# Beside a product-key layer: gates weighed on ScalarE and stored in pieces, table tiles split 56 and 72, and half of the value sums kept in PSUM

## The chip, the cores and the metric

One Trainium2 chip, one of its cores. The kernel is a single program that is launched once; the time is that of the device from the first to the last instruction and what lies around it, in microseconds (us), lower is better. "Before" is the kernel as it stood, "after" the kernel with the change.

## What is computed

The reference is one layer of an encoder: a token-mixing part (a long convolution, a dilated window attention, gates, an output projection and a layer norm), then a product-key retrieval over 16384 experts. Only the second part is touched:

```python
def peer(u, wq, keys, utab, vtab):              # 1024 tokens, width 1024
    q = (xt @ wq).reshape(T, 8, 2, 128)
    s = jnp.einsum('thpe,hpke->thpk', q, keys)
    sv, si = lax.top_k(s, 16)
    cand = (sv[:, :, 0, :, None] + sv[:, :, 1, None, :]).reshape(T, 8, 256)
    cidx = (si[:, :, 0, :, None] * 128 + si[:, :, 1, None, :]).reshape(T, 8, 256)
    tv, ti = lax.top_k(cand, 16)
    eidx = jnp.take_along_axis(cidx, ti, axis=-1)
    g = jax.nn.softmax(tv, axis=-1)
    ...
        a = jnp.einsum('cd,ced->ce', xb, utab[ib])
        coef = gb * jax.nn.gelu(a, approximate=False)
        return jnp.einsum('ce,ced->cd', coef, vtab[ib])
```

So each token has 8 x 16 = 128 chosen experts, each with a gate; the result is the gated sum of their rows of `vtab`, with a coefficient that needs the token's product with their rows of `utab`.

## The kernel before

The kernel treats 256 of the 1024 tokens sparsely (it gathers the chosen rows, one indirect DMA for each of 256 turns, 128 rows of 4 KB each) and 768 densely: for these it multiplies with the whole tables, 128 tiles of 128 experts. Every large product is done three times (`product3`, L79 to L81), since each f32 operand is held as a high and a low part.

Three stages at the end are touched.

**stage_select.** VectorE does the two rounds of top 16, the softmax and the indices for eight blocks of tokens, n = 0 to 7. Beside it TensorE works through the first tiles of `utab` (`se_aps`, 48 matmuls of 384 columns each tile): `AT` = 8 tiles for each block, so 64 in all. ScalarE rounds each tile to its high part (`k_ut_h`), GpSimd subtracts it (`k_ut_l`), ScalarE applies Gelu and stores the result to `scratch_ahead`. VectorE needs one exponential of ScalarE for each block; ScalarE does it behind tile `AT - 2` of the block.

**stage_gates.** TensorE does the other 64 tiles (`ga_aps`) and, beside them, writes the dense gate matrix. For each group of four tokens VectorE builds one-hot rows (`one_hot`): `second` marks the chosen second key, `first` the first key times the gate, in a high and a low f16 part. That is twelve instructions of 128 columns. TensorE multiplies them (eight small matmuls, `ga_ps`), ScalarE writes the group into a block buffer (`ga_wide` or `k_big` in turns), 12 groups to a block, 16 blocks. A whole block goes to `scratch_gates` in one DMA of 3072 KB, whose runs are 48 tokens x 4 B = 192 B long. Each tile has three groups. VectorE also does four products with gathered rows for each tile (`dot`, L1948) and the low part of the next tile (`low`, L1953). ScalarE issues both kinds of stores, `scratch_ahead` (L1908) and `scratch_gates` (L1912), from one queue in program order, and waits at those points like at any other instruction.

**stage_values.** 32 groups of four tiles. For each tile, VectorE multiplies Gelu by gate (`va_c`), ScalarE rounds the product and the tile of `vtab` (`va_c_h`, `va_vt_h`), VectorE makes the low parts (`va_c_l` L2148, `va_vt_l` L2152). TensorE then does, for each of `DT` = 6 tiles of tokens, 24 matmuls of 512 columns over the four tiles of the group, into one of four pairs of PSUM banks; VectorE adds each pair into `k_big` (`add_sums`, L2160): six adds in each group. TensorE starts a group when all four of its tiles are ready (`ready`) and finds a free pair by `f_ok`. On VectorE everything stands in one written order (`turn`): for t = 0 to 3 the product, one add, the two low parts of tile t of the next group, and two or three gathered rows (L2176); then the adds 4 and 5. Two groups are prepared in turns, so group g + 1 is prepared while TensorE does group g. The last two groups are multiplied into PSUM together, and the end adds the rest, the residual and the layer norm for eight tiles of tokens.

## Time and profile before

| | us |
|---|---|
| median of 3 runs | 4294.86 |
| lowest, highest | 4288.96, 4295.96 |
| the profiled execution | 4303.32 |
| its span, first to last instruction | 4301.5 |
| select, as TensorE sees it (1671.2 to 2208.2) | 537.0 |
| gates (2212.5 to 3178.3) | 965.8 |
| values, group 1 to 29 (3254.0 to 4204.6) | 950.6 |
| values, the rest to the end | 96.9 |

Over the span TensorE is busy for 88%, VectorE for 67%, ScalarE for 23% and GpSimd for 30%. These shares are a mean over stages with different limits. Times in the rows count from the span's start. A row of the timeline gives the start, the duration, the engine, the line, the instruction and, in brackets, how long the engine had been idle and who ended that. Instructions overlap with their successor, so what one costs in a chain is the distance from start to start, not the duration.

### The profile page before, as it was taken

What the parts mean: (1) busy time and instruction counts of PE and PEld (TensorE: products, weight loads), DVE (VectorE), ACT (ScalarE), POOL (GpSimd) and SP (SyncE); (2) the same over time, 40 slices, a digit from 0 to 9 for tenths busy, and PEclk for the clock granted to TensorE, in tenths of its full rate; (3) what the DMA queues carried; (4) which work ended last, traced back from release to release, by engine and by line L of the source; (5) the groups of instructions that cost most, each with busy time, mean ns of one, the idle gap of its engine ahead of it and who ended that gap; (6) DMA issues with size and microseconds to landing.
All of it is one profiled execution on the core that took longest, in us unless ns stands there. A gap on an engine that the chain in (4) does not pass through costs nothing. (4 is left out here: it accounts for less than half of the span.)

```text
span 4301.5 us, 57936 instructions
## 1 busy us (share of the span) xinstructions
PE 3764.7 (88%) x19170; PEld 3289.1 (76%) x19170; DVE 2871.9 (67%) x6317; ACT 977.2 (23%) x1361; POOL 1302.5 (30%) x805
## 2 busy tenths in 40 slices
PE   6889899997879798999987776777758999999997
PEld 3579788886757688999986776776757888888885
DVE  5562133224544315788778897988859888888898
ACT  1111122221132211222322222222222222222221
POOL 1132112112312112332333232323215544454450
PEclk9789999998989899999998898988889999999998
DMA  4741212216542223333349989898998787888784
GB/s 183 282 138 41 84 60 80 75 62 223 195 173 96 83 83 102 122 131 119 129 152 259 241 268 236 271 240 258 244 249 319 288 296 287 286 292 300 276 308 153
DMA packets 501996, 826.29 MB, mean 192 GB/s; under 512 B 288455, under 2 KB 309191, under 8 KB 495720
## 3 DMA queue, kind: packets, MB, share of 16 engines
q1 hardware_dynamic: 111848, 370.03, 24.8%
q0 software_dynamic: 84096, 318.80, 20.8%
q10 hardware_dynamic: 305856, 135.28, 13.1%
q8 instruction: 69, 1.13, 0.1%
q14 instruction: 127, 1.04, 0.1%
HBM read 679.31 MB, written 144.70 MB: 192 GB/s over the span
## 5 line engine op out<-in xcount | busy, mean ns | idle before, releaser
L2049 POOL DMA_INDIRECT va_rows<-in_vtab,k_pick x256 | 500.5, 1955 | 531.6 <-DVE k_big L2176 436.5
L79 PE MATMUL va_fps<-va_vt_h,va_c_h 128*128 128x512 f32 x1536 | 601.2, 391 | 53.8 <-DVE va_vt_l L2152 51.4
L80 PE MATMUL va_fps<-va_vt_l,va_c_h 128*128 128x512 f32 x1536 | 600.1, 391 | 0.0
L81 PE MATMUL va_fps<-va_vt_h,va_c_l 128*128 128x512 f32 x1536 | 599.7, 390 | 0.0
L79 PE MATMUL ga_aps<-k_u_h,k_ut_h 128*128 128x384 f32 x1024 | 382.4, 373 | 116.2 <-DVE k_ut_l L1953 112.2
L1941 DVE TENSOR_SCALAR ga_first<-ga_iota,k_sel,ga_gs 128x128 f16<-128x128 f16 x1536 | 427.9, 353 | 33.0 <-issue 33.0
L79 PEld LDWEIGHTS va_fps<-va_vt_h,va_c_h 128*128 128x128 f32 x1536 | 289.9, 189 | 116.9 <-DVE va_vt_l L2152 52.5
L80 PE MATMUL ga_aps<-k_u_l,k_ut_h 128*128 128x384 f32 x1024 | 367.8, 359 | 0.0
L81 PE MATMUL ga_aps<-k_u_h,k_ut_l 128*128 128x384 f32 x1024 | 366.8, 358 | 0.0
L79 PE MATMUL se_aps<-k_u_h,k_ut_h 128*128 128x384 f32 x1024 | 343.8, 336 | 15.2 <-POOL k_ut_l L1619 15.2
L80 PE MATMUL se_aps<-k_u_l,k_ut_h 128*128 128x384 f32 x1024 | 343.2, 335 | 0.0
L81 PE MATMUL se_aps<-k_u_h,k_ut_l 128*128 128x384 f32 x1024 | 343.2, 335 | 0.0
L81 PEld LDWEIGHTS va_fps<-va_vt_h,va_c_l 128*128 128x128 f32 x1536 | 289.9, 189 | 60.6
L80 PEld LDWEIGHTS va_fps<-va_vt_l,va_c_h 128*128 128x128 f32 x1536 | 289.9, 189 | 60.1
L2176 DVE SCALAR_TENSOR_TENSOR k_big<-va_rows,va_coef,k_big 128x1024 f32<-128x1024 f32 x254 | 316.9, 1281 | 17.2 <-DMA va_rows<-in_vtab,k_pick 15.6
L79 PEld LDWEIGHTS ga_aps<-k_u_h,k_ut_h 128*128 128x128 f32 x1024 | 213.9, 209 | 123.2 <-issue 96.8
L1619 POOL TENSOR_TENSOR k_ut_l<-k_ut,k_ut_h 128x1024 fp32r<-128x1024 f32 x65 | 176.3, 2713 | 399.2 <-ACT k_ut_h L1666 399.2
L2160 DVE TENSOR_TENSOR k_big<-k_big,va_fps 128x1024 f32<-128x1024 f32 x174 | 211.5, 1218 | 105.6 <-PE va_fps L81 105.3
L1845 POOL DMA_INDIRECT k_big<-in_urows,k_pick x128 | 170.8, 1335 | 301.0 <-DVE k_big L1948 295.8
L1868 PE MATMUL ga_ps<-ga_first,ga_second 128*128 128x128 f16 x1536 | 126.6, 229 | 135.2 <-DVE ga_first L1941 135.2
L1845 POOL DMA_INDIRECT ga_rows<-in_urows,k_pick x128 | 121.3, 948 | 368.7 <-DVE ga_rows L1948 357.8
L1868 PEld LDWEIGHTS ga_ps<-ga_first,ga_second 128*128 128x128 f16 x1536 | 92.4, 102 | 168.1 <-DVE ga_first L1941 150.0
(293 smaller groups left out, 8173.6 us busy)
## 6 DMA issues: line engine op xcount, KB each, us to landing
k_ut<-in_utab SPq DMA_DIRECT2D x129, 512.0 KB, 3.3
va_vt<-in_vtab SPq DMA_DIRECT2D x128, 512.0 KB, 6.7
va_c<-scratch_ahead SPq DMA_DIRECT2D x128, 384.0 KB, 4.8
va_wt<-scratch_gates SPq DMA_DIRECT2D x128, 384.0 KB, 5.6
hy_tab<-in_tab POOLq DMA_DIRECT2D x64, 512.0 KB, 5.1
sp_wada<-in_w_ada SPq DMA_DIRECT2D x24, 1024.0 KB, 8.8
scratch_ahead<-se_gelu_a ACTq DMA_DIRECT2D x64, 384.0 KB, 2.4
scratch_ahead<-ga_gelu_a ACTq DMA_DIRECT2D x64, 384.0 KB, 4.6
```

Of the source, the lines that this page charges most:

```text
L79: nc.tensor.matmul(out, w[0], x[0], start=first, stop=False)
L80: nc.tensor.matmul(out, w[0], x[1], start=False, stop=False)
L81: return nc.tensor.matmul(out, w[1], x[0], start=False, stop=last)
L1619: nc.gpsimd.tensor_tensor(ut_l[:, s, :, :], ut[:, s, :, :], ut_h[:, s, :, :].bitcast(F32), ALU.subtract).then_inc(ut_ok, 1)
L1845: nc.gpsimd.indirect_dma_start(got[q % SLOTS_G], None, T["urows"], picked(K, q)).then_inc(got_in[q % SLOTS_G], 16)
L1868: last = nc.tensor.matmul(ps[:, e, t * NK:(t + 1) * NK], second[:, e, t, :], first[:, e, part, t, :], start=part == 0, stop=part == 1)
L1941: last = v.tensor_scalar(first[:, b, part, t, :], iota[:, :], K["sel"][:, 0, at], gs[:, part, at], ALU.is_equal, ALU.mult)
L2049: nc.gpsimd.indirect_dma_start(got[:, q % SLOTS_G, :], None, vrows, picked(K, q)).then_inc(got_in[q % SLOTS_G], 16)
L2160: v.tensor_tensor(row, row, banks(DT * s + tt), ALU.add).then_inc(f_ok, 1)
L2176: v.scalar_tensor_tensor(out=sums[:, n, :], in0=got[:, k, :], scalar=share, in1=sums[:, n, :], op0=ALU.mult, op1=ALU.add).then_inc(row_use ...
```

## The change

It does five things.

1. `AT` is 7 instead of 8: select does 56 tiles, gates does 72. The exponential stands behind tile `AT - 3` = 4 of a block instead of 6.
2. In gates, the 192 groups are spread over 72 tiles (4 turns of 18 tiles, 48 groups and 64 gathered rows), so a tile has two or three groups.
3. VectorE writes `second` and a plain `first` (no gate): eight instructions for each group instead of twelve. ScalarE reads the plain row and multiplies it by the low and by the high part of the gate (`weigh`): eight instructions of 128 columns for each group, each with a scale that is read from a column of `gs`. They stand two groups ahead of the group that ScalarE writes out.
4. A finished block is stored in four DMAs of 768 KB (same 192 B runs), one behind each of the next four tiles' stores to `scratch_ahead`. The last block is cut as before.
5. In values, three of the six tiles of tokens (`STAY` = 3, tt = 0, 1, 2) stay in three pairs of PSUM banks for the whole stage and are never added by VectorE. The other three pass through the fourth pair, one after the other. TensorE alternates: passing 0, staying 0, passing 1, staying 1, passing 2, staying 2. VectorE has three adds in a group, at t = 0, 1, 2, and none at t = 3. In the residual a staying tile needs one instruction instead of two, and all residual steps now come after the last `turn`.

```diff
-AT = 8
+AT = 7
...
-                        if j == AT - 2:
+                        if j == AT - 3:
                             act.wait_ge(e_in, n + 1)
...
+            def weigh(m):
+                act.wait_ge(hot_ok, m + 1)
+                b = m % 4
+                for part in (1, 0):
+                    for t in range(G):
+                        at = m * G + t
+                        last = nc.scalar.activation(first[:, b, part, t, :], first[:, b, 0, t, :], ACT.Copy,
+                                                    scale=gs[:, part, at:at + 1])
+                last.then_inc(f_ok, 1)
...
+            for n in range(BESIDE):
+                i, q, a = n // TILES, n % TILES, n % 2
+                split(1 - a, n + 1, n // 2)
+                act.wait_ge(act_stored[a], 16 * (n // 2 + 1))
+                todo = list(groups_of(q))
+                for h in range(2):
+                    gelu(a, n, h)
+                    for b in (todo[:-1], todo[-1:])[h]:
+                        m = GROUPS * i + b
+                        if m + AHEAD < BLOCKS * BLOCK:
+                            weigh(m + AHEAD)
+                        if m % BLOCK == 0 and m // BLOCK >= 2:
+                            hold(act, K, stored[m // BLOCK % 2], 16 * PIECES * (m // BLOCK // 2))
+                        scatter_out(m)
+                        if m % BLOCK == BLOCK - 1 and m // BLOCK < BLOCKS - 1:
+                            waiting += [(m // BLOCK, c, m) for c in range(PIECES)]
+                act.wait_ge(gelu_ok, 2 * n + 6)
+                act.dma_start(S["ahead"][n + FIRST], gelu_a[:, a, :]).then_inc(act_stored[a], 16)
+                if waiting:
+                    block, c, m = waiting.pop(0)
+                    act.wait_ge(act_out, m + 5)
+                    store(block, NK // PIECES * c, NK // PIECES * (c + 1), stored[block % 2])
...
                 for t in range(G):
                     at = bass.ds(m * G + t, 1)
                     v.tensor_scalar(second[:, b, t, :], iota[:, :], K["sel"][:, 1, at], None, ALU.is_equal)
-                    for part in range(2):
-                        last = v.tensor_scalar(first[:, b, part, t, :], iota[:, :], K["sel"][:, 0, at],
-                                               gs[:, part, at], ALU.is_equal, ALU.mult)
-                last.then_inc(f_ok, 1)
+                    last = v.tensor_scalar(first[:, b, 0, t, :], iota[:, :], K["sel"][:, 0, at], None, ALU.is_equal)
+                last.then_inc(hot_ok, 1)
...
+            def group(s, g):
+                ready(g)
+                for j in range(STAY):
+                    passing(s, g, j)
+                    last = staying(s, j, False)
+                last.then_inc(group_mm, 1)
...
                 for t in range(GT):
                     coefficients(g + 1, t)
-                    add(t)
+                    if t < STAY:
+                        add(t)
                     coef_low(1 - s, g + 1, t)
                     value_low(1 - s, g + 1, t)
                     for j in range(take * t, take * t + take):
                         take_row(start, j, isinstance(start, int) and start == 0 and j < GATHERED)
-                for tt in range(GT, DT):
-                    add(tt)
...
             for t in range(GT):
                 coefficients(NG - 1, t)
-                residual(DT - GT + t)
+                residual(t)
                 coef_low(1, NG - 1, t)
                 value_low(1, NG - 1, t)
```

ScalarE in gates, one tile with three groups. L1883 is the rounding of the next tile, L1893 Gelu, L1887 the writing out of a group. Before:

```order
L1883 ACTIVATE k_ut_h<-k_ut 128x1024
L1892 REGISTER_ALU
L1893 ACTIVATE ga_gelu_a<-ga_aps 128x384
L72 ISA
L1887 ACTIVATE ga_wide<-ga_ps 128x128x4
L72 REGISTER_ALU
L1887 ACTIVATE ga_wide<-ga_ps 128x128x4
L1892 REGISTER_ALU
L1893 ACTIVATE ga_gelu_a<-ga_aps 128x384
```

The same place after (L1893 is now the rounding, L1904 Gelu, L1916 the weighing, L1898 the writing out, L1942 and L1907 the two stores):

```order
L1893 ACTIVATE k_ut_h<-k_ut 128x1024
L1904 ACTIVATE ga_gelu_a<-ga_aps 128x384
L1916 ACTIVATE ga_first<-ga_first,ga_gs 128x128 x8
L1898 ACTIVATE ga_wide<-ga_ps 128x128x4
L1916 ACTIVATE ga_first<-ga_first,ga_gs 128x128 x8
L1898 ACTIVATE ga_wide<-ga_ps 128x128x4
L1904 ACTIVATE ga_gelu_a<-ga_aps 128x384
L1916 ACTIVATE ga_first<-ga_first,ga_gs 128x128 x8
L1898 ACTIVATE ga_wide<-ga_ps 128x128x4
L1942 DMA scratch_ahead<-ga_gelu_a 128x768
L1907 DMA scratch_gates<-k_big 128x32x48
```

Eight weighing instructions stand before each writing out, and a piece of a block behind the tile's own store.

VectorE in values, the second half of the turn of group 1 (t = 2 and 3, three gathered rows each). Before, with L2160 the add:

```order
L2144 TENSOR_TENSOR va_c<-va_c,va_wt 128x768
L2160 TENSOR_TENSOR k_big<-k_big,va_fps 128x1024
L2148 TENSOR_TENSOR va_c_l<-va_c,va_c_h 128x768
L2152 TENSOR_TENSOR va_vt_l<-va_vt,va_vt_h 128x1024
L2176 SCALAR_TENSOR_TENSOR k_big<-va_rows,va_coef,k_big 128x1024 x3
L2160 TENSOR_TENSOR k_big<-k_big,va_fps 128x1024 x2
```

That is t = 3 with the adds 4 and 5 behind it. After, t = 2 and t = 3, with L2212 the add:

```order
L2196 TENSOR_TENSOR va_c<-va_c,va_wt 128x768
L2212 TENSOR_TENSOR k_big<-k_big,va_fps 128x1024
L2200 TENSOR_TENSOR va_c_l<-va_c,va_c_h 128x768
L2204 TENSOR_TENSOR va_vt_l<-va_vt,va_vt_h 128x1024
L2228 SCALAR_TENSOR_TENSOR k_big<-va_rows,va_coef,k_big 128x1024 x3
L2196 TENSOR_TENSOR va_c<-va_c,va_wt 128x768
L2200 TENSOR_TENSOR va_c_l<-va_c,va_c_h 128x768
L2204 TENSOR_TENSOR va_vt_l<-va_vt,va_vt_h 128x1024
```

The last add of a group stood behind the low parts of the group's last tile (t = 3); now it stands ahead of the low parts of t = 2 and t = 3.

## Rows read from the trace of the kernel before

**Rows 1.** Windows by stage: length, busy time (and count) by engine, PEclk, DMA share, GB/s.

```profile
1671.20:2208.20 537.00, 537.00 (x3087) 536.80 (x3088) 441.24 (x1635) 155.11 (x220) 173.88 (x64) 0.99 0.35 122
2212.50:3178.30 965.80, 718.18 (x4608) 678.39 (x4608) 838.25 (x2883) 236.98 (x383) 292.15 (x256) 0.88 0.92 249
3254.00:4204.60 950.60, 948.76 (x4176) 784.80 (x4176) 829.58 (x767) 218.90 (x232) 481.25 (x243) 1.00 0.82 295
```

**Rows 2.** Waits in gates: who waited for whom, us, times, longest.

```profile
ACT k_ut_h L1883 <- issue: 203.0, 29, 23.0
```

**Rows 3.** Timeline of VectorE in gates.

```profile
2619.87 0.26 DVE L1939 TENSOR_SCALAR ga_second<-ga_iota,k_sel 128x128 f16<-128x128 f16 x1
2620.04 0.54 DVE L1941 TENSOR_SCALAR ga_first<-ga_iota,k_sel,ga_gs 128x128 f16<-128x128 f16 x2
2620.48 0.26 DVE L1939 TENSOR_SCALAR ga_second<-ga_iota,k_sel 128x128 f16<-128x128 f16 x1
```

**Rows 4.** Timeline of ScalarE in gates (ACTq is its issue of a DMA).

```profile
2633.86 0.39 ACTq L1912 DMA_DIRECT2D scratch_gates<-ga_wide  x1
...
2644.72 23.30 ACTq L1908 DMA_DIRECT2D scratch_ahead<-ga_gelu_a  x1
2668.16 1.06 ACT L1883 ACTIVATE k_ut_h<-k_ut 128x1024 fp32r<-128x1024 f32 x1 [23.01 <-issue]
2669.12 0.47 ACT L1893 ACTIVATE ga_gelu_a<-ga_aps 128x384 f32<-128x384 f32 x1
2669.49 1.08 ACT L1887 ACTIVATE k_big<-ga_ps 128x512 f32<-128x512 f32 x2
```

**Rows 5.** Timeline of TensorE in gates, one group of eight small matmuls.

```profile
2632.26 0.62 PE L1868 MATMUL ga_ps<-ga_first,ga_second 128*128 128x128 f16 x8
2632.69 0.42 PE L79 MATMUL ga_aps<-k_u_h,k_ut_h 128*128 128x384 f32 x1
```

**Rows 6.** Groups of ScalarE by form: busy us, mean ns, idle before; then its timeline.

```profile
L799 ACT ACTIVATE at_out_c<-at_cps 128x512 f32<-128x512 f32 x56 | 33.2, 593 | 110.6 <-PE at_cps L81 110.6
L797 ACT ACTIVATE at_conv<-at_cps,at_cb,at_cw 128x512 f32<-128x512 f32 x24 | 18.7, 778 | 84.5 <-PE at_cps L81 84.5
L1684 ACT ACTIVATE se_e<-se_e 128x128 f32<-128x128 f32 x8 | 2.5, 312 | 0.1
...
1356.06 2.91 ACT L1341 ACTIVATE k_big<-ou_tps,k_ada_col 128x128 f32<-128x128 f32 x8 [17.09 <-PE ou_tps L1312]
```

**Rows 7.** DMA in 2656:2668 (GB/s in 40 slices), then the packets in 2760:2772.

```profile
GB/s 233 258 174 153 144 145 145 302 90 299 372 429 429 198 260 195 150 145 145 156 233 229 372 401 428 254 261 237 151 145 145 145 146 144 147 145 144 145 145 146
...
DMA packets 10878, 3.85 MB, mean 321 GB/s; under 512 B 10424, under 2 KB 10424, under 8 KB 10878
```

**Rows 8.** Timeline of VectorE in values, first steps of one turn.

```profile
3719.55 1.22 DVE L2160 TENSOR_TENSOR k_big<-k_big,va_fps 128x1024 f32<-128x1024 f32 x1 [3.36 <-PE va_fps L81]
3720.69 0.95 DVE L2148 TENSOR_TENSOR va_c_l<-va_c,va_c_h 128x768 fp32r<-128x768 f32 x1
3721.56 1.22 DVE L2152 TENSOR_TENSOR va_vt_l<-va_vt,va_vt_h 128x1024 fp32r<-128x1024 f32 x1
3722.70 2.48 DVE L2176 SCALAR_TENSOR_TENSOR k_big<-va_rows,va_coef,k_big 128x1024 f32<-128x1024 f32 x2
3725.09 0.95 DVE L2144 TENSOR_TENSOR va_c<-va_c,va_wt 128x768 f32<-128x768 f32 x1
```

**Rows 9.** Timeline of VectorE at the start of values, with no add between.

```profile
3200.41 0.96 DVE L2144 TENSOR_TENSOR va_c<-va_c,va_wt 128x768 f32<-128x768 f32 x1 [18.22 <-DMA va_wt<-scratch_gates]
3202.28 0.96 DVE L2148 TENSOR_TENSOR va_c_l<-va_c,va_c_h 128x768 fp32r<-128x768 f32 x1 [0.91 <-ACT va_c_h L2119]
```

**Rows 10.** Timeline of TensorE in values, behind a wait.

```profile
3254.03 0.79 PE L79 MATMUL va_fps<-va_vt_h,va_c_h 128*128 128x512 f32 x1 [9.05 <-DVE va_vt_l L2152]
```

**Rows 11.** Windows of the four us from 3252, same columns as rows 1.

```profile
3252.00:3256.00 4.00, 1.97 (x5) 1.58 (x6) 4.00 (x4) 1.06 (x1) 0.56 (x1) 0.50 1.02 366
3256.00:3260.00 4.00, 4.00 (x16) 3.26 (x15) 4.00 (x5) 0.00 (x0) 3.10 (x3) 0.82 0.99 358
```

More of the change, by code:

```diff
@@ L1915, in _, with store @@
-            with act.Fori(0, BLOCKS // 2 - 1) as i:
-                tile(i, False)
-            tile(BLOCKS // 2 - 1, True)
-            act.wait_ge(stored[0], 16 * (BLOCKS // 2 + 1))
+            def store(block, lo, hi, done):
+                act.dma_start(S["gates"].rearrange("i j t -> j i t")[:, lo:hi, block * TW:(block + 1) * TW],
+                              wide[block % 2][:, lo:hi, :]).then_inc(done, 16)
+            def weigh(m):
[7 more added lines that the diff above has]
+                last.then_inc(f_ok, 1)
@@ L1919, in _ @@
+            assert not waiting
+            act.wait_ge(act_out, BLOCKS * BLOCK + 4)
+            for c, (lo, hi) in enumerate(((0, 2), (2, 8), (8, NK))):
+                store(BLOCKS - 1, lo, hi, K["last_gates"][c])
+            act.wait_ge(stored[0], 16 * PIECES * (BLOCKS // 2))
+            act.wait_ge(stored[1], 16 * PIECES * (BLOCKS // 2 - 1))
             for s in range(2):
@@ L1954, in low @@
                                 ALU.subtract).then_inc(ut_ok, 1)
-            def quarter(i, q, more):
-                n = 4 * i + q
-                for b in range(PER):
-                    one_hot(PER * n + b, (PER * q + b) % 4)
-                    dot(n, b)
-                if more:
-                    low(1 - q % 2, n + 1)
-                dot(n, PER)
-            with dve.Fori(0, TURNS - 1) as i:
-                for q in range(4):
-                    quarter(i, q, True)
-            for q in range(4):
-                quarter(TURNS - 1, q, q < 3)
+            with dve.Fori(0, TURNS) as i:
+                for q in range(TILES):
+                    for b in groups_of(q):
+                        one_hot(GROUPS * i + b, b % 4)
+                        for j in rows_after(b):
+                            dot(i, j)
+                    low(1 - q % 2, TILES * i + q + 1)
 def stage_values(nc, S, K, T, out):
@@ L2002, in stage_values, with banks @@
         vrows = T["vtab"].rearrange("i j d -> (i j) d")
-        order = [GATHERED + tt for tt in range(DT)] + list(range(GATHERED))
-        last_order = list(range(GATHERED)) + [GATHERED + tt for tt in range(DT)]
+        STAY = DT // 2
+        FINAL = [STAY, 0, STAY + 1, 1, STAY + 2, 2]
+        order = [GATHERED + tt for tt in FINAL] + list(range(GATHERED))
+        last_order = list(range(GATHERED)) + [GATHERED + tt for tt in FINAL]
+        def banks(tt):
+            pair = tt if tt < STAY else STAY
+            return fps[:, 2 * pair:2 * pair + 2, :]
         @block.sync
@@ L2052, in _, with part, passing, staying @@
         def _(pe):
-            pe.sem_inc(f_mm, 2 * DT)
-            def part(s, t, tt, bank, h, first, last):
-                return product3(nc, fps[:, 2 * bank + h, :],
+            pe.sem_inc(group_mm, 2)
+            def part(s, t, tt, h, first, last, into=None):
+                return product3(nc, banks(tt if into is None else into)[:, h, :],
                                 (c_h[:, s, t, tt * P:(tt + 1) * P], c_l[:, s, t, tt * P:(tt + 1) * P]),
                                 (vt_h[:, s, t, half(h)], vt_l[:, s, t, half(h)]), first, last)
-            def group(s, g):
-                for tt in range(DT):
-                    pe.wait_ge(f_ok, DT * g + tt + 1)
-                    for h in range(2):
-                        for t in range(GT):
-                            last = part(s, t, tt, (DT * s + tt) % BP, h, t == 0, t == GT - 1)
-                    last.then_inc(f_mm, 1)
+            def passing(s, g, j):
+                pe.wait_ge(f_ok, STAY * g + j + 1)
+                for h in range(2):
+                    for t in range(GT):
+                        last = part(s, t, STAY + j, h, t == 0, t == GT - 1)
+                return last.then_inc(f_mm, 1)
+            def staying(s, tt, last_group):
+                for h in range(2):
+                    for t in range(GT):
+                        last = part(s, t, tt, h, False, last_group and t == GT - 1)
+                return last
             def ready(g):
@@ L2104, in _ @@
                         for t in range(GT):
-                            last = part(s, t, tt, tt % BP, h, s == 0 and t == 0, s == 1 and t == GT - 1)
-                last.then_inc(f_mm, 1)
+                            last = part(s, t, tt, h, s == 0 and t == 0, s == 1 and t == GT - 1, into)
+                return last
+            staying(1, STAY, True).then_inc(done_mm, 1)
+            staying(1, 0, True).then_inc(done_mm, 1)
+            pe.wait_ge(done_ok, 1)
+            both(STAY + 1, STAY).then_inc(done_mm, 1)
+            staying(1, 1, True).then_inc(done_mm, 1)
+            pe.wait_ge(done_ok, 2)
+            both(STAY + 2, 0).then_inc(done_mm, 1)
+            staying(1, 2, True).then_inc(done_mm, 1)
         @block.scalar
@@ L2229, in _ @@
             hold(dve, K, row_used, GATHERED * PICKS + SLOTS_G)
-            for k in range(DT, KT):
+            for k in range(GT, KT):
                 residual(k)
```

167 lines of the change are left out of this document (81 added, 86 removed).

## The prediction

> **What bounds the kernel now.** I read first the windows by stage. In select and in values TensorE is busy without a gap at the full granted clock: 537.0 us for 64 tiles, 8.39 us each, and 950.6 us for 29 groups, 32.8 us each [rows 1]. In gates it is not: the same 64 tiles take 965.8 us, 15.1 us each, VectorE is busy for 838 us of it, the DMA engines for 0.92 and ScalarE for a quarter. The waits say what the rest is. ScalarE stood 203 us at points where no other engine held it up [rows 2], and its timeline shows the point: it issues the 3072 KB store of a block, and the second DMA that it issues behind it takes 23.3 us to be taken [rows 4]. Then the rounding of the next tile is late, and VectorE and TensorE are dry. So gates is VectorE's written work (about 13 us a tile) and one such stall in most blocks.
>
> **Select, fewer tiles.** TensorE has eight tiles less: 8 x 8.39 = -67 us [rows 1]. What is late next is VectorE, with 441 us busy in this stage [rows 1], 55 a block, some 57 with its small gaps, against TensorE's new 58.7. It fits by less than 2 us a block, and the exponential that now comes two tiles earlier keeps VectorE from waiting. If VectorE were 2 us slower than I read it, 8 us of the 67 come back.
>
> **Gates, VectorE.** A one-hot instruction without a gate is 0.17 us from start to start, a pair with gates 0.44 [rows 3], so a token falls from 0.61 to 0.34. For all: 768 x 0.34 = 261, 256 products of about 1.2 (as the gathered rows in [rows 8]) = 307, 72 low parts of 1.14 = 82, in sum 650 us. VectorE stops being the bound.
>
> **Gates, ScalarE.** It gets 1536 instructions of 128 columns. None like them is in the trace. An instruction of 128 columns with constants lasts 0.312, and one of 512 with two column operands 0.778 against 0.593 without, 0.09 for each operand [rows 6]. Successors overlap: Gelu of 0.47 is followed after 0.37, rounding of 1.06 after 0.96 [rows 4]. So 0.312 + 0.09 - 0.10 = 0.30. Low bound 0.21, if the operand hides; high bound 0.36, since eight with two operands took 2.91 [rows 6]. I take 0.30, because it is built from the nearest row in width. The Trainium skill (ScalarE: Activation LUTs, What ACT_TABLE_LOAD costs) gives 186 ns + 0.833 ns per column, about 93 for each operand and 93 of overlap; by it the sum would have 0.293, and the rows above agree. A tile on ScalarE is then 0.96 rounding + 2 x 0.37 Gelu + 2.67 x 0.48 writing out + 0.75 for two issues of 0.4 (the second not in each tile) = 3.7, plus 21.3 x 0.30 = 6.4: 10.1 us, 730 us for 72 tiles, and some 13 us until the first tiles run. ScalarE goes from a quarter to the fullest engine.
>
> **Gates, TensorE.** 72 x 8.39 = 604, and 192 groups of small matmuls at 0.43 [rows 5] = 83: 687, 700 with the start. It lies beside ScalarE's 743.
>
> **Gates, DMA.** A store with nothing beside it runs at 145 GB/s [rows 7]; 15 blocks of 3.146 MB need 325 us so. The rest (256 gathers and 72 table tiles of 0.524 MB, 72 stores of 0.393) is 200 MB, at the 400 GB/s and more of the best slices [rows 7] 500 us. One after the other this is 825 us, more than ScalarE needs. But they overlap: in the 12 us of the second row 10424 small packets (13.8 us by the rate above) and 1.85 MB of others (4.6 us) went through, 18.4 in 12 [rows 7]. So bounds of 540 and 825. From the share itself, 249 GB/s at 0.92 [rows 1], 248 MB would need 915. I expect no clean bound but some friction: 768 KB pieces take about a tile's time beside the gathers, so now and then an issue on ScalarE still waits, a few us instead of 23. The cutting removes most of the stalls; I add 47 us (0.65 a tile) for what is left. Gates is then 790 us instead of 965.8: **-176 us**. Ends: 700 (TensorE, short weighing), 841 (weighing at 0.36), 915 (share).
>
> **Values, the new chain.** TensorE's matmuls are the same, and it had no gap, so VectorE's three spared adds per group (3.4 us) are spare time that nobody waits for. But the order costs. Group g + 1 may start when the low parts of its t = 3 are done, and on VectorE these stand behind the third add of group g. That add needs passing tile 2, which ends after 5/6 of the group: 27.3 us in. Before, the add ahead of t = 3 was number 3, which ends after 4/6 (21.9). From the third add on, read off start to start: reaction 0.4, add 1.14, `va_c_l` 0.87, `va_vt_l` 1.14, two gathered rows 2.39 [rows 8], the product of t = 3 and ScalarE's rounding until `va_c_l` 1.87 [rows 9], which is open here since no add stands between, `va_c_l` 0.87, `va_vt_l` 1.22. Sum 9.9 us. Cover is only staying tile 2, 5.5 us. So TensorE waits: 27.3 + 9.9 = 37.2 for a group instead of 32.8, **4.4 us** each time.
>
> A wait of this kind also costs clock. After the 9.05 us wait of [rows 10] the granted clock is 0.50 (1.2 GHz) for the rest of one window and 0.82 in the next [rows 11], together about 3.4 us at half speed, 1.7 us lost; in gates it was the same after most waits over 3 us (mean clock 0.88 in [rows 1]). I take 1.5 per group; the ends are 0 and 1.8. A group is then 38.7 us, +5.9. The prepared groups are 2 to 31: turns 2 to 27 give 26 x 5.9 = 153; turns 1, 28 and 29 take three gathered rows, 1.2 more, 3 x 7.1 = 21. The start (fewer matmuls for each first tile, longer wait for the DMA, the first copy no earlier) I put at +2. In the end VectorE spares three adds and three residual multiplications, but all residual steps now stand behind the last turn, and SyncE's loads of the last two tiles stand behind the waits for the first residuals: +5. **+181 us** in all, 130 without the clock loss.
>
> **The sum.** Against the profiled execution of 4303.3: 4303.3 - 67 - 176 + 181 = 4241. That execution is 8.4 above the median, so **4233 us**, 1.4% less.
>
> **The rivals.** (a) *The DMA engines become the bound of gates.* For: share 0.92 already, and the stage is to be a fifth shorter with 7 MB more. Against: the 12 us above, and stretches without a store at far less. Then ScalarE's issues and VectorE's gathers wait, gates is 870 to 915, and the time 4313 to 4358: slower. It decides from a gates stage of about 850. The Trainium skill (DMA: Bandwidth & Descriptors, Issuing engines are not separate DMA queues) says that transfers of all issuing engines share the same 16 and interleave; that is this rival's premise, and the rows on share agree. (b) *The wait in values is short of clock loss*, or VectorE gets ahead more than I see (gathered rows and rounding hidden): +130, time about 4182. (c) *Weighing is cheaper*, 0.21 to 0.25, TensorE is the bound of gates at 700 to 730: 4145 to 4175. (d) *The change does not bring the chain*: TensorE stays gapless in values, gain of both other stages kept, 4303 - 67 - 176 - 8 = 4052. Against it stands the written order, which has no way around the third add.
>
> **How the numbers follow.** Chances: forecast (gates 760 to 830, values +160 to +190) 0.47; (a) 0.20; (b) 0.18; (c) 0.11; (d) 0.04. The forecast's own range is 4195 to 4275. The range that should hold 8 in 10 leaves out (d), the upper third of (a) and the lower part of (c): 4160 to 4330. A difference of under 0.2% (8.6 us) is about what a measurement of this kernel cannot tell from none. Faster by more: the forecast, (b), (c), (d), less a little of the forecast's upper edge, 0.76. Slower by more: most of (a) and a little of the forecast, 0.18. Between: 0.06.
>
> **What would show it.** Select about 470 us, TensorE gapless; a transposition waiting for VectorE would show my margin wrong. In gates ScalarE busy for some 700 of 790 us, the weighing group at 0.30 from start to start, issues of a few us at most, TensorE's waits on ScalarE or on the low parts. In values TensorE waits on `va_vt_l` about 30 times, 4 to 5 us each, once a group, with the clock at 0.5 behind it and a mean of about 0.95; VectorE idle ahead of its third add. The prediction is wrong if values takes about 33 us a group, or if gates is over 850 with the DMA share at 1.

## The result and the profile after

| | before | after |
|---|---|---|
| median of 6 runs | 4294.7 us | 4255.27 us |
| lowest to highest | 4283.53 to 4297.56 | 4248.54 to 4268.09 |
| profiled execution | 4303.32 | 4264.03 |

The ratio is 0.9918, with a 95% interval of 0.9899 to 0.9937: 0.8% faster. That is 22 us more than the 4233 forecast, inside its own range (4195 to 4275). Two large effects of opposite sign stand behind the small number, and the windows by stage show them. The columns are those of [rows 1]: stretch, length, busy time of TensorE's matmuls and weight loads, VectorE, ScalarE and GpSimd, granted clock, DMA share, GB/s. In order: select, gates, values group 1 to 29, the rest.

```profile
1676.60:2146.60 470.00, 470.00 (x2702) 469.72 (x2703) 439.48 (x1635) 138.70 (x196) 145.42 (x56) 0.99 0.35 124
2151.20:2943.90 792.70, 720.32 (x4984) 689.09 (x4984) 638.28 (x2125) 669.95 (x1939) 295.24 (x256) 0.96 1.07 313
3020.10:4162.10 1142.00, 1012.73 (x4176) 823.82 (x4176) 734.05 (x680) 220.22 (x233) 360.08 (x243) 0.93 0.72 245
4162.10:4262.20 100.10, 71.46 (x288) 57.77 (x288) 78.72 (x96) 9.25 (x16) 0.00 (x0) 0.86 0.34 127
```

Against [rows 1]: select 537.0 to 470.0, gates 965.8 to 792.7, the 29 groups of values 950.6 to 1142.0. In select TensorE has no gap still. In gates ScalarE is now the second fullest engine (237 us before, 670 now), and VectorE has fallen from 838 to 638. In values TensorE is busy for 1013 of 1142 us, at a mean clock of 0.93, where it had no gap before.

The waits (total us, times, longest) name what is late. The first two lines are from the gates stage, and the second of them answers to [rows 2]; the other two are from the whole program:

```profile
ACT ga_first L1916 <- DVE ga_first L1975: 84.8, 44, 10.4
...
ACT k_ut_h L1893 <- issue: 12.8, 8, 2.9
...
DVE k_big L2212 <- PE va_fps L81: 381.1, 87, 5.6
...
PE va_fps L79 <- DVE va_vt_l L2204: 176.0, 33, 28.9
```

ScalarE's stalls at the rounding, 203.0 us before [rows 2], are 12.8 us. Its largest wait is now for VectorE's plain one-hot rows, 84.8 us. In values TensorE waits 33 times for the low part of a table tile: once for each group, and the others at the start of the stage, where the longest, 28.9 us, stands. VectorE itself waits for TensorE ahead of 87 adds. Each engine waits for the other in turn: a chain that goes through both.

The timeline of one tile on ScalarE in gates (start, duration, engine, line, instruction, how many; `ACTq` is its queue that issues DMAs) shows the new work:

```profile
2499.07 1.06 ACT L1893 ACTIVATE k_ut_h<-k_ut 128x1024 fp32r<-128x1024 f32 x1 [0.25 <-issue]
2500.04 0.47 ACT L1904 ACTIVATE ga_gelu_a<-ga_aps 128x384 f32<-128x384 f32 x1
2500.41 2.44 ACT L1916 ACTIVATE ga_first<-ga_first,ga_gs 128x128 f16<-128x128 f16 x8
2502.75 0.58 ACT L1898 ACTIVATE ga_wide<-ga_ps 128x512 f32<-128x512 f32 x1
...
2506.94 1.27 ACTq L1907 DMA_DIRECT2D scratch_gates<-ga_wide  x1
...
2509.24 1.06 ACT L1893 ACTIVATE k_ut_h<-k_ut 128x1024 fp32r<-128x1024 f32 x1
```

Eight weighings take 2.34 us from start to the start of what follows, 0.293 each; a full tile takes 2509.24 - 2499.07 = 10.17 us. The piece of the block (L1907) is issued in 1.27 us while the weighings go on. The next DMA behind a piece, a store to `scratch_ahead`, takes 6.93 us at most in this stage, where the one behind the uncut block took 23.3 [rows 4].

And the starts of four successive groups in values on TensorE, with the wait ahead of each in brackets:

```profile
3178.39 0.79 PE L79 MATMUL va_fps<-va_vt_h,va_c_h 128*128 128x512 f32 x1 [4.34 <-DVE va_vt_l L2204]
3218.24 0.79 PE L79 MATMUL va_fps<-va_vt_h,va_c_h 128*128 128x512 f32 x1 [4.34 <-DVE va_vt_l L2204]
3256.99 0.79 PE L79 MATMUL va_fps<-va_vt_h,va_c_h 128*128 128x512 f32 x1 [4.34 <-DVE va_vt_l L2204]
3296.80 0.79 PE L79 MATMUL va_fps<-va_vt_h,va_c_h 128*128 128x512 f32 x1 [4.34 <-DVE va_vt_l L2204]
```

A group takes 39.85, 38.75, 39.81 us. 32.8 of work and 4.34 of wait make 37.1; the rest, 2.7 and 1.6 in turn, is time at the lower clock. The windows behind the first of these waits show it, the clock being the third number from the end:

```profile
3174.00:3178.00 4.00, 0.05 (x1) 0.00 (x0) 3.09 (x4) 1.90 (x2) 2.15 (x2) 0.88 0.82 251
3178.00:3182.00 4.00, 3.61 (x9) 2.85 (x10) 3.51 (x4) 0.45 (x1) 1.98 (x2) 0.50 0.97 333
3182.00:3186.00 4.00, 4.00 (x15) 3.22 (x14) 0.00 (x0) 1.30 (x2) 0.71 (x1) 0.76 1.00 391
3186.00:3190.00 4.00, 4.00 (x20) 3.30 (x19) 3.14 (x3) 0.15 (x1) 0.00 (x0) 1.00 0.09 35
```

### The profile page after: what moved, and what is told of

Its sections match the earlier page's. It is cut to its first block and busy times, and to the rows that moved or that the text cites. A ratio compares the mean times of both kernels' runs of the same rounds, so it can differ in the third digit from the quotient of the medians.

```text
span 4262.2 us, 57381 instructions
## 1 busy us (share of the span) xinstructions
PE 3770.9 (88%) x19170; PEld 3277.4 (77%) x19170; DVE 2565.5 (60%) x5465; ACT 1396.8 (33%) x2897; POOL 1153.5 (27%) x797
## 5 line engine op out<-in xcount | busy, mean ns | idle before, releaser
L79 PE MATMUL va_fps<-va_vt_h,va_c_h 128*128 128x512 f32 x1536 | 631.1, 411 | 184.6 <-DVE va_vt_l L2204 176.0
L2082 POOL DMA_INDIRECT va_rows<-in_vtab,k_pick x256 | 377.3, 1474 | 850.4 <-DVE k_big L2228 748.0
L79 PEld LDWEIGHTS va_fps<-va_vt_h,va_c_h 128*128 128x128 f32 x1536 | 305.6, 199 | 262.9 <-issue 164.6
L1916 ACT ACTIVATE ga_first<-ga_first,ga_gs 128x128 f16<-128x128 f16 x1536 | 470.2, 398 | 85.0 <-DVE ga_first L1975 84.8
L79 PE MATMUL ga_aps<-k_u_h,k_ut_h 128*128 128x384 f32 x1152 | 404.6, 351 | 27.9 <-issue 20.8
L2171 ACT ACTIVATE va_c_h<-va_c 128x768 fp32r<-128x768 f32 x128 | 108.1, 845 | 790.1 <-DVE va_c L2196 790.1
L2212 DVE TENSOR_TENSOR k_big<-k_big,va_fps 128x1024 f32<-128x1024 f32 x87 | 106.2, 1221 | 381.1 <-PE va_fps L81 381.1
L79 PE MATMUL se_aps<-k_u_h,k_ut_h 128*128 128x384 f32 x896 | 301.1, 336 | 15.6 <-POOL k_ut_l L1619 15.6
L80 PE MATMUL se_aps<-k_u_l,k_ut_h 128*128 128x384 f32 x896 | 300.3, 335 | 0.0
L81 PE MATMUL se_aps<-k_u_h,k_ut_l 128*128 128x384 f32 x896 | 300.3, 335 | 0.0
L79 PEld LDWEIGHTS ga_aps<-k_u_h,k_ut_h 128*128 128x128 f32 x1152 | 221.2, 192 | 38.1 <-issue 30.2
L80 PEld LDWEIGHTS ga_aps<-k_u_l,k_ut_h 128*128 128x128 f32 x1152 | 222.0, 193 | 0.0
L81 PEld LDWEIGHTS ga_aps<-k_u_h,k_ut_l 128*128 128x128 f32 x1152 | 220.8, 192 | 0.0
```

Of the source, the lines that this page charges most:

```text
L79: nc.tensor.matmul(out, w[0], x[0], start=first, stop=False)
L80: nc.tensor.matmul(out, w[0], x[1], start=False, stop=False)
L81: return nc.tensor.matmul(out, w[1], x[0], start=False, stop=last)
L1916: last = nc.scalar.activation(first[:, b, part, t, :], first[:, b, 0, t, :], ACT.Copy, scale=gs[:, part, at:at + 1])
L2082: nc.gpsimd.indirect_dma_start(got[:, q % SLOTS_G, :], None, vrows, picked(K, q)).then_inc(got_in[q % SLOTS_G], 16)
L2171: nc.scalar.activation(c_h[:, s, t, :], c[:, t % 2, :], ACT.Copy).then_inc(c_hi, 1)
```

## The experiments

Theory: gates gains by two things that are both needed, the cut (no stall at ScalarE's issue) and the weighing on ScalarE (VectorE no longer the bound); values loses by the place of the third add, in part as wait, in part as clock. Rivals: one of the two parts of gates brings the gain alone; the transfers bound gates; TensorE waits in values for the single passing pair of banks, not for the order on VectorE; the time beyond the wait isn't clock.

All runs in one table. "Gates" and "values" are the times from the first to the last start of the first product of the stage (L79), so that they read alike for all; the ratio is to before.

| kernel | median us | ratio, 95% | gates | values |
|---|---|---|---|---|
| before | 4294.7 | | 964.5 | 1079.8 |
| after | 4255.27 | 0.9918 [0.9899, 0.9937] | 791.9 | 1274.6 |
| e1 values alone | 4492.87 | 1.0470 [1.0441, 1.0498] | 959.8 | 1279.8 |
| e2 rest alone | 4061.15 | 0.9465 [0.9439, 0.9492] | 793.3 | 1076.9 |
| e3 third add at t = 3 | 4080.47 | 0.9526 [0.9505, 0.9548] | 786.9 | 1098.5 |
| e4 product ahead | 4086.49 | 0.9533 [0.9507, 0.9559] | 789.8 | 1109.8 |
| e5 whole block | 4433.48 | 1.0322 [1.0301, 1.0343] | 966.7 | |
| e6 constant scale | 4244.86 | 0.9879 [0.9856, 0.9902] | 778.1 | |
| e7 extra copy | 4314.84 | 1.0061 [1.0037, 1.0084] | 857.4 | |
| e8 fill the wait | 4199.92 | 0.9768 [0.9748, 0.9789] | 794.7 | 1220.8 |
| e9 cut alone | 4337.35 | 1.0101 [1.0083, 1.0119] | 868.4 | |
| e10 whole block from SyncE | 4557.21 | 1.0600 [1.0575, 1.0625] | 1088.7 | |
| e11 rest alone, pieces from SyncE | 4173.34 | 0.9718 [0.9703, 0.9733] | 905.7 | 1075.7 |

### One half of the change at a time

e1 is the kernel before with only the new `stage_values`; e2 is the changed kernel with the old `stage_values`.

> The kernel before with the change's stage_values alone (three tiles of tokens stay in PSUM, three pass through one pair). Theory: the third add stands ahead of the low parts of t = 2 and t = 3, so TensorE waits 4.3 to 5.5 us once a group and its clock falls behind each wait: group 1 to 29 takes 1142 us instead of 950.6, the kernel about 4295 + 191 = 4486. Rival: the longer values stage of the change comes from what gates leaves behind (DMA queues, semaphores, order of memory), then values alone stays near 33 us a group and the kernel near 4295.

> The change without its stage_values (adds of all six tiles on VectorE, two pairs alternating, as before). Theory: select and gates keep all of their gain, group 1 to 29 is 951 us again, the kernel about 4255 - 191 = 4064, and gates is 793 us as in the change. Rival: the parts depend on each other, the gain is less than 230 us against the kernel before.

e1 is 205 us slower than before, which was measured again beside it at 4287.67, and e2 226 us faster. The halves add up to -21 us, against the -39 of both together. Of these 18 us, 5 lie in values (1279.8 and 1274.6); where the rest lies wasn't traced, and the runs of before alone spread over 14 us. The waits of TensorE, of e1 and of e2:

```profile
PE va_fps L79 <- DVE va_vt_l L2177: 175.3, 33, 26.2
```

```profile
PE va_fps L79 <- DVE va_vt_l L2179: 46.6, 7, 26.8
```

So the 33 waits belong to the new values and to nothing else, and e2, with select and gates as changed and values as before, is the fastest of all kernels here: 5.4% less than before, 4.6% less than after.

### Is it the place of the third add?

e3 moves one add on VectorE; matmuls, banks and their order stay.

```diff
-                    if t < STAY:
-                        add(t)
+                    if t in (0, 1, 3):
+                        add((0, 1, None, 2)[t])
```

> The change with one edit: VectorE's third add of a group stands at t = 3 instead of t = 2, behind the product and ahead of the low parts of the last tile, where it also covers ScalarE's rounding. Theory (order): from the second add (16.8 us) on, the low parts of t = 3 are done at 32.6 to 33 us, so TensorE waits less than 0.5 us in most groups and about 2.5 in the three with three gathered rows, without clock loss in the others: 33.0 us a group, the kernel 4064 to 4085. Rival (bank): it is the one passing pair that TensorE cannot refill in time; a later third add would make that worse, 39 us a group or more, 4255 or slower.

A hit: 4080.47 us, 175 less than after. The waits of TensorE that are left in the groups are three of 2.2 us, each behind a turn with three gathered rows; the others stand at the start and at the end. The three, and two of the end:

```profile
3043.86 0.49 PE L79 MATMUL va_fps<-va_vt_h,va_c_h 128*128 128x512 f32 x1 [2.25 <-DVE va_vt_l L2204]
3933.25 0.49 PE L79 MATMUL va_fps<-va_vt_h,va_c_h 128*128 128x512 f32 x1 [2.25 <-DVE va_vt_l L2204]
3968.35 0.50 PE L79 MATMUL va_fps<-va_vt_h,va_c_h 128*128 128x512 f32 x1 [2.17 <-DVE va_vt_l L2204]
4001.47 0.80 PE L79 MATMUL va_fps<-va_vt_h,va_c_h 128*128 128x512 f32 x1 [11.06 <-DVE va_vt_l L2204]
4022.98 0.80 PE L79 MATMUL va_fps<-va_vt_h,va_c_h 128*128 128x512 f32 x1 [7.41 <-DVEq L2290]
```

The single passing pair isn't what costs: with the same banks, values falls from 1274.6 to 1098.5. The order on VectorE is 176 of the 195 us that the new values costs. Of the 19 left, the groups, with the three waits, make 11 and the end 10, and the start is 2 shorter. A gain over the old values (1079.8) isn't there: three spared adds on an engine that nobody waits for bring nothing.

e4 goes on from e3 and puts the product of tile t + 1 ahead of the gathered rows of t, to shorten the chain in the three-row groups too.

> As the run with the third add at t = 3, and the product of tile t + 1 stands ahead of the gathered rows of tile t, so ScalarE's rounding is always covered. Theory: the low parts of t = 3 end 1 to 3 us earlier, no wait in any group, 32.8 us a group, the kernel at 4055 to 4070, up to 15 us less than with the add moved alone. Rival (bank): as there, no better than 4255.

A miss: 4086.49 us, no better than e3 (the intervals overlap), and values is 11 us longer. VectorE's timeline ahead of the same group, first e3, then e4, shows where it went:

```profile
3935.30 2.60 DVE L2228 SCALAR_TENSOR_TENSOR k_big<-va_rows,va_coef,k_big 128x1024 f32<-128x1024 f32 x2 [0.98 <-DMA va_rows<-in_vtab,k_pick]
```

```profile
3934.22 1.28 DVE L2228 SCALAR_TENSOR_TENSOR k_big<-va_rows,va_coef,k_big 128x1024 f32<-128x1024 f32 x1 [4.50 <-DMA va_rows<-in_vtab,k_pick]
```

VectorE came to a gathered row sooner and waited 4.50 us for it instead of 0.98. In all, these waits were 41.5 us in 34 places, and TensorE's waits behind the same three turns are 5.2 to 6.4 us instead of 2.2. Why the rows themselves came no earlier wasn't tested.

### Is the rest of a group clock?

e8 is the changed kernel; where TensorE would wait, it does 18 matmuls that nothing reads, into the passing pair.

```diff
+                pe.wait_ge(f_ok, STAY * g + STAY + 1)
+                for t in range(GT):
+                    last = part(s, t, STAY, 0, True, True)
+                for t in range(2):
+                    last = part(s, t, STAY, 1, True, True)
                 last.then_inc(group_mm, 1)
```

> The changed kernel; in each group of the values stage TensorE does 18 unneeded matmuls of the same form (about 3.9 us at full clock) into the passing pair, at the place where it otherwise waits 4.34 us for the residue of the next tile. Nothing reads their sums. My theory: a group took 39.3 us, 6.5 over the 32.8 us of work, 4.34 of it the wait itself and about 2.1 us the lower clock after it. With the wait filled the granted clock stays up, the group takes 37.0 to 37.8 us, and the stage of 29 groups 45 to 65 us less: time 4190 to 4215 us. Rival: the 2.1 us are not the clock but the matmuls' own queueing or a longer chain on VectorE: then the group stays at 39 us or grows with the added work, time 4250 to 4310 us.

A hit: 4199.92 us, 55 less than after, with more work. The starts of three groups and two windows of about a group:

```profile
3207.32 0.49 PE L79 MATMUL va_fps<-va_vt_h,va_c_h 128*128 128x512 f32 x1 [0.27 <-DVE va_vt_l L2209]
3244.59 0.49 PE L79 MATMUL va_fps<-va_vt_h,va_c_h 128*128 128x512 f32 x1 [0.27 <-DVE va_vt_l L2209]
3281.88 0.49 PE L79 MATMUL va_fps<-va_vt_h,va_c_h 128*128 128x512 f32 x1 [0.27 <-DVE va_vt_l L2209]
```

```profile
3170.00:3207.00 37.00, 36.98 (x162) 30.33 (x162) 24.52 (x23) 7.50 (x8) 13.99 (x8) 1.00 0.76 252
3207.00:3244.60 37.60, 37.06 (x164) 30.36 (x163) 25.15 (x25) 7.79 (x9) 13.12 (x8) 1.00 0.75 254
```

The clock is 1.00 in these windows and a group takes 37.28 us, against the 37.2 that the prediction's chain gives without any clock loss. So of the 39.3 us, 32.8 are work, 4.4 the chain, and 2.1 clock.

### Gates: the cut, the weighing, or both?

e5 stores a block in one piece again (`PIECES = 1`). e9 keeps the four pieces and gives the weighing back to VectorE (ScalarE has no `weigh` and no calls of it):

```diff
...
-                    last = v.tensor_scalar(first[:, b, 0, t, :], iota[:, :], K["sel"][:, 0, at], None, ALU.is_equal)
-                last.then_inc(hot_ok, 1)
+                    for part in range(2):
+                        last = v.tensor_scalar(first[:, b, part, t, :], iota[:, :], K["sel"][:, 0, at],
+                                               gs[:, part, at], ALU.is_equal, ALU.mult)
+                last.then_inc(f_ok, 1)
```

> The changed kernel with the block of gates stored in one piece of 3072 KB again, everything else as changed. My theory: the 203.0 us that ScalarE waited at its transpose in the kernel before were time in which it stood at the issue of a store behind the uncut one; with ScalarE now the bound of the gates (669.95 us busy of 792.7), these waits come back on the path: eight blocks by up to 23 us less what the other engines absorb, so the gates stage takes 60 to 170 us more, 850 to 960 us, and the time is 4315 to 4425 us. Rival: the cut is worth nothing, because the weighing on ScalarE and the removed row weighing on VectorE brought the gain alone: the gates stage stays within 15 us of 793 us and the time within 15 us of 4255 us.

> The changed kernel, but VectorE makes the weighed one-hot rows again (twelve instructions for each group, as in the kernel before) and ScalarE weighs nothing; the block stays cut in four pieces. The uncut block with ScalarE's weighing gave a gates stage of 967 us, as long as before, so the weighing alone brought nothing. My theory: both are needed. With the cut alone VectorE is the bound, 768 tokens x 0.61 = 468, 256 products 307, 72 low parts 82, in sum 857 us, with some friction 870 to 910 us for the stage, 75 to 115 us more than as changed: time 4330 to 4370 us. Rival: the cut brings the whole gain, the stage stays within 15 us of 793 us, time 4240 to 4270 us.

e5: 4433.48 us, a little above its range, gates 966.7, the length of before. ScalarE's waits are back, 198.8 us. First the total, then one of them with the issue that made it:

```profile
ACT k_ut_h L1893 <- issue: 198.8, 14, 19.2
```

```profile
2325.25 0.45 ACTq L1907 DMA_DIRECT2D scratch_gates<-ga_wide  x1
2335.03 19.89 ACTq L1942 DMA_DIRECT2D scratch_ahead<-ga_gelu_a  x1
2355.02 1.06 ACT L1893 ACTIVATE k_ut_h<-k_ut 128x1024 fp32r<-128x1024 f32 x1 [17.20 <-issue]
```

The 3072 KB store is issued in 0.45 us. The next DMA of the same queue, 9.8 us later, takes 19.89 us to be issued, and the rounding behind it starts as it ends. The Trainium skill (Perfetto Trace Analysis, Per-instruction lifecycle: what the profiler-reported window actually captures) says that such a row covers the sequencer's work with the descriptor generator and not the movement of the data; by that it is the sequencer that stands still here, and the trace agrees: ScalarE goes on as the row ends. How long the row is, is set by the store ahead: such a store takes 29.5 us from its issue to its landing in e5, and this row ends 29.7 us after the store's issue.

e9: 4337.35 us, gates 868.4, both in the expected range. Its window:

```profile
2143.80:3012.80 869.00, 738.80 (x4986) 700.88 (x4987) 845.58 (x2891) 257.90 (x406) 325.96 (x256) 0.96 1.01 286
```

VectorE is busy for 846 of 869 us: with the stalls gone it is the bound, close to the 857 us that the sum of its instructions gave. So the two parts do not simply add:

| gates, us | weighing on VectorE | on ScalarE |
|---|---|---|
| whole block | 964.5 (64 tiles) | 966.7 |
| four pieces | 868.4 | 791.9 |

Three of the cells have 72 tiles. Among these the cut brings 175 us where ScalarE weighs, and the weighing on ScalarE brings 77 where the block is cut. The first cell has eight tiles less (67 us of TensorE in select). So moving the weighing without the cut paid for no more than these eight tiles, and the cut without it brought 96 us although it carried them. What each would bring alone at 64 tiles wasn't run.

### What bounds gates now?

e6 weighs with a constant (`scale=1.0`), so that the gates are missing from the result; e7 adds a copy of 512 KB for each tile, issued by SyncE.

> The changed kernel, but ScalarE's weighing multiplies by the constant 1.0 and not by the gate in memory: the same rows are read and written, the weighting of the table rows by the gates is left out. My theory: ScalarE is the bound of the gates, and a row costs it 0.293 us because the multiplier is read per partition (VectorE's 0.16 us for the plain row hides behind it). With a constant a row takes about 0.20 us, a tile on ScalarE falls from 10.17 to about 8.2 us, TensorE with its 690 to 720 us becomes the bound, and the gates stage takes 715 to 745 us: 50 to 75 us off, time 4180 to 4210 us. Rival: another engine or the transfers bound the stage (DMA or VectorE): the stage stays within 15 us of 793 us. A second rival: the row costs the same with a constant, then nothing moves either, but the mean of one weighing stays at 0.29 us.

> The changed kernel, and in the gates stage SyncE also copies one table tile of 512 KB from memory to memory for each tile of the stage, 38 MB more in all, that nothing reads. My rival from the prediction was that the transfers bound the stage; the engines' mean share reads 1.07 at 313 GB/s, which speaks for it. If they did, 38 MB beside the 248 MB would cost about 15 percent, 90 to 120 us more: time 4345 to 4375 us. My theory, that ScalarE bounds it: the transfers fit in, the stage grows by less than 20 us, time 4255 to 4275 us.

Neither bears out my theory that ScalarE alone is the bound: e6 ends at the edge of its rival's range, and e7 between theory and rival. e6: the weighing did get cheaper, eight in 1.59 us, 0.20 each, and ScalarE's busy time fell by 132 us; the stage fell by 14. The stage of e6, and two rows of its ScalarE:

```profile
2137.00:2916.00 779.00, 718.29 (x4984) 690.66 (x4984) 636.81 (x2124) 537.87 (x1932) 302.27 (x256) 0.96 1.08 318
```

```profile
2462.01 1.69 ACT L1916 ACTIVATE ga_first<-ga_first 128x128 f16<-128x128 f16 x8
2463.60 0.58 ACT L1898 ACTIVATE ga_wide<-ga_ps 128x512 f32<-128x512 f32 x1
```

TensorE is busy for 718 of 779 us. ScalarE waits more for everyone: 106.5 us for VectorE's plain rows (84.8 in after), 52.5 at the issue (12.8), 46.4 for TensorE's products (11.8). The last two lines are waits of TensorE itself, with nothing in the profile that it waited for:

```profile
ACT ga_first L1916 <- DVE ga_first L1975: 106.5, 63, 10.7
ACT k_ut_h L1893 <- issue: 52.5, 22, 5.2
ACT ga_gelu_a L1904 <- PE ga_aps L81: 46.4, 47, 5.5
...
PE ga_aps L79 <- issue: 21.9, 3, 7.9
...
PE ga_aps L81 <- issue: 9.6, 3, 3.9
```

These two, 31.5 us, are half of the 61 us that TensorE is not busy. They stand at tiles 18, 36 and 54, where a new turn of the loop of 18 tiles begins, and after has them at the same places (20.8 and 8.0 us). The kernel before, with turns of 4 tiles, has no such wait of TensorE. Why TensorE stands there wasn't tested. Most of the other half, 26.7 us, are waits for the weighed rows.

e7: the stage takes 65 us more, with 37 MB more. If all transfers were the bound, 15% of 792 would be 119 us; if none, nothing. ScalarE's wait at the issue went from 12.8 to 69.2 us, which is about the size of the loss:

```profile
2130.00:2988.50 858.50, 735.86 (x4987) 701.63 (x4988) 637.71 (x2125) 672.78 (x1942) 291.04 (x256) 0.94 1.09 333
```

```profile
ACT k_ut_h L1898 <- issue: 69.2, 30, 6.7
```

So gates stands near several limits at once: ScalarE's 670 us, TensorE's 720, the transfers, whose load it feels as longer issues on ScalarE, and the written order between VectorE and ScalarE. In after ScalarE waits 84.8 us for VectorE's rows, and VectorE 100.3 us for ScalarE's rounding of the next tile, ahead of which it can't go on to the next rows. Taking 132 us off ScalarE brings 14; loading the transfers costs at once. Another order on VectorE wasn't tried.

### Is it the queue or the engines?

e10 is e5 with the whole block issued by SyncE, behind its load of the next but one tile; e11 is e2 with the four pieces issued by SyncE.

```diff
...
+            for n in range(1, BESIDE):
+                load(n % 2, n)
+                for block, c, m in stores.get(n, []):
+                    sp.wait_ge(act_out, m + 5)
+                    lo, hi = NK // PIECES * c, NK // PIECES * (c + 1)
+                    sp.dma_start(S["gates"].rearrange("i j t -> j i t")[:, lo:hi, block * TW:(block + 1) * TW],
+                                 wide[block % 2][:, lo:hi, :]).then_inc(stored[block % 2], 16)
...
```

> The changed kernel with the block stored in one piece of 3072 KB, as in the run with the whole block, but issued by SyncE behind its load of the next but one table tile, not by ScalarE. My theory: what cost 174 us there was the place of the stall, not the transfer: ScalarE stood at the issue of the next small store for up to 23 us. On SyncE the next table load is what stands behind, it comes one tile (10 us) later by itself and is needed a tile after that, so most is hidden: ScalarE's waits without a cause fall from 198.8 to under 20 us, the stage takes 800 to 870 us, time 4260 to 4340 us. Rival: the uncut store keeps the 16 DMA engines from the other transfers, whoever issues it: the stage stays at 940 to 970 us, and the waits are at transfers (table tiles, gathered rows).

> Select and gates as changed, values as before (the run that gave 4061.15), and the four pieces of a block issued by SyncE behind its table loads instead of by ScalarE. If ScalarE's busy time and its queue bound the gates, 60 issues of 0.39 us and the waits behind them (12.8 us) fall away: the stage takes 760 to 785 us instead of 793, time 4030 to 4055 us. If the transfers or TensorE bound it, nothing changes, 4055 to 4070 us. If a table load comes late behind a piece, it is slower: 4070 to 4100 us, with TensorE or ScalarE waiting for the table tile.

Both missed in time, and e10 tells most. As my theory had it, ScalarE's waits at the issue are gone. But the stage takes 1088.7 us, more than with the stall, and the wait is at the table tile. The total, how long the stores take from issue to landing (the last number), and one of the waits:

```profile
ACT k_ut_h L1903 <- DMA k_ut<-in_utab: 347.7, 15, 27.4
```

```profile
scratch_gates<-ga_wide SPq DMA_DIRECT2D x8, 3072.0 KB, 24.9
```

```profile
2350.48 0.40 SPq L1855 DMA_DIRECT2D scratch_gates<-ga_wide  x1
2350.85 0.36 ACTq L1952 DMA_DIRECT2D scratch_ahead<-ga_gelu_a  x1
2350.92 25.79 SPq L1841 DMA_DIRECT2D k_ut<-in_utab  x1
2380.93 1.06 ACT L1903 ACTIVATE k_ut_h<-k_ut 128x1024 fp32r<-128x1024 f32 x1 [27.29 <-DMA k_ut<-in_utab]
```

In the same microsecond ScalarE issues its own store in 0.36 us, while the load on SyncE's queue, behind the big store, takes 25.79. This load is taken 26.2 us after the store's issue, about when the store has landed. ScalarE's own store has moved its last packet 5.7 us after its issue, in the middle of the big one. So the store holds up what stands behind it in its own queue, and hardly anything else: the stage has no wait for a gathered row, which GpSimd issues. That is against the rival that the engines are full, though the rival had named late table tiles too. The Trainium skill (DMA: Bandwidth & Descriptors, Queues, rings and completion order) says that each of the 16 engines goes round between the queues that have work for it; this run agrees, by the small store that passed the big one. That a transfer is late by the order of its own queue is my reading of the two rows on SyncE's queue. What I had wrong is the price: I counted on the load coming a tile later with a tile of slack, but it comes 25.8 us later, and ScalarE waits 23.2 us for each of the 15 stores (347.7 / 15); the stage grows by 19.8 us for each. On ScalarE the same stall came 10 us later, behind work that was still queued, and made 14 waits of 14.2 us (198.8 / 14); the stage grew by 11.7 for each store. e11 is the same in small: pieces in SyncE's queue make the table tiles late, and the stage takes 905.7 instead of 793.3. Its largest such line:

```profile
ACT k_ut_h L1903 <- DMA k_ut<-in_utab: 148.9, 16, 11.1
```

## Why the prediction was right, point by point

- **Select, -67.** Measured 67.0. The margin of 2 us a block for VectorE held, TensorE has no gap.
- **Gates, -176 (790 us).** Measured -173.1 (792.7). The prices of the work held: VectorE 638 against 650, a weighing 0.293 against 0.30, ScalarE's work 670 us against 673 (72 tiles of 10.1 less the 0.75 for issues). That the stage came out within 3 us is luck in part. The 54 us for issues are not there: the issues run beside the weighings, and the 10.17 us of the tile above are the work of three groups alone, where my 10.1 was a mean tile of 2.67 groups with its issues. The 47 us of friction, which I expected as longer issues, are mostly something else: ScalarE waits 12.8 us at the issue, but 84.8 for VectorE's plain rows (10.4 of it at the start), a wait that is in no term of mine. The reason that I gave, ScalarE as the single bound, is only partly right: e6 took 132 us off it, and the stage fell by 14. Rival (c), cheaper weighing with 700 to 730 for the stage, was therefore priced too low: even at 0.20 the stage takes 778. The step at fault is "700 with the start", which has none of the waits (some 29 us of them at the seams of the loop) and none of the clock loss (0.96, with TensorE busy for 720 us where I had 687) that TensorE has in this stage.
- **Gates, DMA, rival (a).** The stage ran with a share of 1.07, and came out at 793, below the 825 of one transfer after the other. The share was no measure of a bound: 313 GB/s now against 249 [rows 1]. Yet e7 shows that the rival was near: 15% more traffic would have eaten 65 of the 173 us.
- **The cut "removes most of the stalls".** It does, 203.0 to 12.8, and e5 and e9 show that it is what the gain hangs on.
- **Values, the chain, 4.4 us.** Measured 4.34 in ordinary groups, 5.5 in those with three rows (5.6 by the prediction). e3 and e8 show the cause and the length, 37.28 us against 37.2.
- **Values, the clock, 1.5 us a group.** The term that was mis-sized: 2.1, above my upper end of 1.8. I took it from one wait of 9 us, with 3.4 us at half speed behind it [rows 11]. Behind the 4.34 us waits the clock is low for some 5.5 us in one group (0.50, then 0.76 in the windows above) and for some 3.2 in the next. A shorter wait did not cost less. With the three-row groups it makes 191.4 us against the 174 of the sum, 17 of the 23 us by which the profiled execution (4264.0) missed the 4241. With start and end values came to +191, just above the +160 to +190 of the forecast.
- **Rival (b), "130 without the clock loss".** The 130 has the groups alone; with the 7 us for start and end the terms give 138, and a time of about 4190 instead of 4182. e8, where the clock stays up in the groups, took 4199.92.
- **Start and end of values.** -3.6 where I had +2, +3.2 where I had +5. In the end there is a wait that I had not foreseen, 8.56 us until VectorE has emptied a bank that TensorE wants for a passing tile; it costs little, since VectorE has work all the while and waits only 0.41 us for what TensorE does behind it:

```profile
4215.30 0.79 PE L79 MATMUL va_fps<-va_vt_h,va_c_h 128*128 128x512 f32 x1 [8.56 <-DVEq L2290]
```

- The rest of the miss: 5.4 us before select, in code that is the same, and 4.1 us between gates and values.

## What to carry to other kernels

Ask of every spared instruction whether anyone waited for it, and of every reordering which last step now stands behind a later event: the three spared adds were worth nothing, and the new place of the last add cost 176 us. Cut a store of many short runs, and look at what is issued behind it in the same queue, because that is what it delays, whichever engine issues it. Two fixes for one stage do not add up: here the one paid little without the other. Price them together, and price the next engine with its waits, not with its busy time.

## What was unexpected of the hardware

- A wait of 4.34 us costs TensorE another 2.1 us by clock, and alternates between 1.6 and 2.7 from group to group. Filling the wait with matmuls that nobody needs made the kernel 1.3% faster.
- The DMA behind a 3072 KB store of 192 B runs takes 19.9 to 25.8 us to be issued, while another engine's issue in the same microsecond takes 0.36.
- At three seams between turns of a loop of 18 written-out tiles, TensorE stands for 7 us and 2 to 3 more (28.8 us in the gates stage of after), with nothing in the profile to wait for.
- The profile's DMA share read 1.07 to 1.09 in stages that still took more traffic (333 GB/s in e7 against 313).
- A scale from a column instead of a constant costs ScalarE 0.09 us for each instruction of 128 columns (0.293 against 0.20 from start to start).
